# Expert gate and up weights read as runs of consecutive rows, with token features and router weights permuted to match

## The reference, cut to what matters

```
m = rmsnorm(h[:, LEAD_PAD:], g_ffn[layer])              # the token rows, width 1024
grp = argmax(softmax(m @ w_rg + b_rg))                  # 4 groups
top_val, top_idx = top_k((m @ w_re + b_re)[grp], 2)     # 2 of the 8 experts of the group
for every (token, expert e) chosen:
    hb = silu(xb @ w_gate[e]) * (xb @ w_up[e])          # 1024 -> 512, 32 experts
    y  = (hb @ w_down[e]) * gate                        # 512 -> 1024
```

## Time and profile before

| | |
|---|---|
| Median of the runs | 2676.31 us |
| Profiled execution, first to last instruction | 2682.0 us (nothing around the span is recorded) |
| TensorE busy, of the span | 2241.3 us (84%) |
| VectorE, ScalarE, GpSimd busy | 1577.4, 1063.9, 433.0 us |
| Mean granted TensorE clock | 0.872 |
| DMA | 346.55 MB in 251273 packets |

### The profile page before, as it was taken

How to read it: one execution, slowest core, us unless ns; L and a number is a source line. 1 busy time by engine, 2 the same in 40 slices (tenths; PEclk the granted TensorE clock), 3 DMA queues, 4 the chain that set the end, 5 groups by cost and what they waited for, 6 DMA issues and landing times. The chain is left out here.

```text
span 2682.0 us, 27601 instructions
## 1 busy us (share of the span) xinstructions
PE 2241.3 (84%) x10272; PEld 1841.8 (69%) x10272; DVE 1577.4 (59%) x1629; ACT 1063.9 (40%) x1243; POOL 433.0 (16%) x310
## 2 busy tenths in 40 slices
PE   6998966757999999992897787886488986899997
PEld 5885655656777787772776677765467865688786
DVE  4114578356788788884249999999733244333312
ACT  3224531215677676773243324433343222322211
POOL 0002121001111111110134454343300011000000
PEclk9996557858999999996798988888689998899999
DMA  4210000407999999984232222222023221333321
GB/s 144 73 48 1 1 0 1 167 32 248 324 342 361 333 356 365 357 316 145 51 95 78 64 63 79 79 63 64 0 89 84 94 94 32 87 95 96 107 79 63
DMA packets 251273, 346.55 MB, mean 129 GB/s; under 512 B 13951, under 2 KB 149623, under 8 KB 250151
## 3 DMA queue, kind: packets, MB, share of 16 engines
q1 hardware_dynamic: 240432, 332.49, 37.3%
q0 software_dynamic: 5200, 8.40, 1.0%
q10 hardware_dynamic: 5543, 4.34, 0.5%
HBM read 341.19 MB, written 12.65 MB: 132 GB/s over the span
## 5 line engine op out<-in xcount | busy, mean ns | idle before, releaser
L1335 DVE TENSOR_TENSOR wlo_e<-raw_e,whi_e 128x2048 fp32r<-128x2048 f32 x192 | 432.1, 2292 | 83.6 <-ACT whi_e L1269 83.6
L47 PE MATMUL pall<-hT_hi,w_lo 128*128 128x512 f32 x864 | 354.7, 411 | 53.2 <-DVE yT L2181 33.6
L1646 ACT CAST w_hi<-w_raw 128x2048 fp32r<-128x2048 f32 x89 | 169.5, 1904 | 540.9 <-PE pall L49 540.9
L1654 DVE TENSOR_TENSOR w_lo<-w_raw,w_hi 128x2048 fp32r<-128x2048 f32 x75 | 171.8, 2291 | 352.6 <-ACT w_hi L1646 352.6
L1269 ACT CAST whi_e<-raw_e 128x2048 fp32r<-128x2048 f32 x192 | 357.2, 1914 | 0.0
L48 PE MATMUL pall<-hT_lo,w_hi 128*128 128x512 f32 x864 | 348.1, 403 | 0.0
L49 PE MATMUL pall<-hT_hi,w_hi 128*128 128x512 f32 x864 | 346.5, 401 | 0.0
L2193 DVE SCALAR_TENSOR_TENSOR mixed<-yT,cols,mixed 128x512 f32<-128x512 f32 x240 | 251.2, 1047 | 7.6
L47 PEld LDWEIGHTS pall<-hT_hi,w_lo 128*128 128x128 f32 x864 | 170.4, 197 | 93.5 <-DVE yT L2181 36.4
L47 PE MATMUL pall<-whi_e,xT_lo 128*128 128x512 f32 x512 | 204.6, 400 | 9.6 <-DVE wlo_e L1335 9.6
L49 PE MATMUL pall<-whi_e,xT_hi 128*128 128x512 f32 x512 | 201.2, 393 | 0.0
(11 more groups left out here) (443 smaller groups left out, 4440.0 us busy)
## 6 DMA issues: line engine op xcount, KB each, us to landing
raw_e<-in_w_expert_up_dram SPq DMA_DIRECT2D x64, 1024.0 KB, 8.2
raw_e<-in_w_expert_down_dram SPq DMA_DIRECT2D x64, 1024.0 KB, 7.6
raw_e<-in_w_expert_gate_dram SPq DMA_DIRECT2D x64, 1024.0 KB, 7.1
w_raw<-in_w_in_dram SPq DMA_DIRECT2D x80, 512.0 KB, 5.4
w_raw<-in_w_gate_up_dram SPq DMA_DIRECT2D x44, 512.0 KB, 5.1
w_raw<-in_w_down_dram SPq DMA_DIRECT2D x22, 512.0 KB, 3.9
mixed<-in_w_in_dram SPq DMA_DIRECT2D x10, 1024.0 KB, 5.0
A<-acs_rows SPq DMA_DIRECT2D x8, 1024.0 KB, 4.9
```

What stands on the lines that cost most here:

```text
L47: nc.tensor.matmul(out, w_lo, m_hi, start=start, stop=False)
L1335: ins = nc.vector.tensor_tensor(wlo[j][:, :], raw[j][:, :], whi[j][:, :].bitcast(F32), ALU.subtract)
L1646: self.nc.scalar.copy(self.hi[i][:, :], self.raw[i][:, :]).then_inc(self.s_hi, 1)
L1654: (engine or self.nc.vector).tensor_tensor(self.lo[i][:, :], self.raw[i][:, :], self.hi[i][:, :].bitcast(F32), ALU.subtract).then_inc(self ...
```

## The change: what it does

Gate and up weights are seen as (p k) f: feature row 8p+k lies on partition p. A unit is half of what a partition holds of the matrix: four consecutive rows, one run of 8 KB. The load of a unit is still one DMA of 1 MB with the same issuer, the same wait and the same place in the program. To match, `xn` is written with its columns in the order k-major (column k*128+p of `xn` is feature 8p+k), so `m_rows`, `xg` and the transposes hold permuted features, and the router weights `wr` are loaded as (p k) c. The overflow block gets the same layout.

The core of the diff (in the third block, the gate and up loads are written in the same way):

```diff
-    w_gate = dram["w_expert_gate"][0].rearrange("e (k p) f -> p e k f", p=P)
-    w_up = dram["w_expert_up"][0].rearrange("e (k p) f -> p e k f", p=P)
+    w_gate = dram["w_expert_gate"][0].rearrange("e (p k) f -> p e (k f)", p=P)
+    w_up = dram["w_expert_up"][0].rearrange("e (p k) f -> p e (k f)", p=P)
     def unit_source(e, j):
         if j < 4:
             w = w_gate if j < 2 else w_up
-            k = 4 * (j % 2)
-            return w[:, bass.ds(e, 1), k:k + 4, :].rearrange("p o k f -> p (o k) f")
+            c = UNIT * (j % 2)
+            return w[:, bass.ds(e, 1), c:c + UNIT].rearrange("p o f -> p (o f)")
     def load(sp, j, of):
-        place = raw_e[j][:, :].rearrange("p (k c) -> p k c", k=4 if j < 4 else 2)
+        place = raw_e[j][:, :] if j < 4 else raw_e[j][:, :].rearrange("p (k c) -> p k c", k=2)
-            act.dma_start(wr[:, :, N_GROUPS:NR], dram["w_router_expert"][0].rearrange("(k p) c -> p k c", p=P)).then_inc(s["wr"], 16)
+            act.dma_start(wr[:, :, N_GROUPS:NR], dram["w_router_expert"][0].rearrange("(p k) c -> p k c", p=P)).then_inc(s["wr"], 16)
+            def fanned(t):
+                return t.rearrange("p (q k) -> p k q", k=KD)
+            def strips(t):
+                return t.rearrange("p (k q) -> p k q", k=KD)
-                nc.vector.scalar_tensor_tensor(xn[i % 2][:, :], h[:, i, :], rs[:, i:i + 1], gbc[:, :], ALU.mult,
-                                               ALU.mult).then_inc(s["xn"], 1)
+                nc.vector.scalar_tensor_tensor(strips(xn[i % 2][:, :]), fanned(h[:, i, :]), rs[:, i:i + 1], fanned(gbc[:, :]),
+                                               ALU.mult, ALU.mult).then_inc(s["xn"], 1)
```

More of the change, by code:

```diff
@@ L961, in _ @@
             act.dma_start(gbc[:, :], dram["g_ffn"][0].partition_broadcast(P)).then_inc(s["gbc"], 16)
-            act.dma_start(wr[:, :, 0:N_GROUPS], dram["w_router_group"][0].rearrange("(k p) c -> p k c", p=P)).then_inc(s["wr"], 16)
-            act.dma_start(wr[:, :, N_GROUPS:NR], dram["w_router_expert"][0].rearrange("(k p) c -> p k c", p=P)).then_inc(s["wr"], 16)
+            act.dma_start(wr[:, :, 0:N_GROUPS], dram["w_router_group"][0].rearrange("(p k) c -> p k c", p=P)).then_inc(s["wr"], 16)
+            act.dma_start(wr[:, :, N_GROUPS:NR], dram["w_router_expert"][0].rearrange("(p k) c -> p k c", p=P)).then_inc(s["wr"], 16)
             act.dma_start(rb[:, 0:N_GROUPS], dram["b_router_group"][0].partition_broadcast(P)).then_inc(s["rb"], 16)
@@ L1520, in turn @@
                 e = sp.value_load(over_e[0:1, bass.ds(j, 1)] if later(j) else over_e[0:1, 0:1], min_val=0, max_val=N_EXPERTS - 1)
-                for w, t in ((w_gate, wg), (w_up, wu), (w_down, wd)):
-                    sp.dma_start(t[:, :, :], w[:, bass.ds(e, 1), :, :].rearrange("p o k f -> p (o k) f")).then_inc(s["w"], 16)
+                for w, t in ((w_gate, wg), (w_up, wu)):
+                    sp.dma_start(t[:, :, :].rearrange("p k f -> p (k f)"),
+                                 w[:, bass.ds(e, 1), :].rearrange("p o f -> p (o f)")).then_inc(s["w"], 16)
+                sp.dma_start(wd[:, :, :], w_down[:, bass.ds(e, 1), :, :].rearrange("p o k f -> p (o k) f")).then_inc(s["w"], 16)
             blocks(sp, turn)
```

## The result

The changed kernel took 2690.11 us (median of four runs, 2689.75 to 2692.58), the kernel before 2676.58 us beside it: a ratio of 1.0052, 95% interval 1.0038 to 1.0067. It is slower by 13.5 us between the medians, and by 13.9 us going by the ratio. The forecast was slower by 32 us. The direction and the place were right, the size was not.

A forecast was written before the change was run, and what follows sets the result against it. The prediction took the late landing of the gather, which TensorE waits for, to bound the expert loop. Span 2682.0 + 31 (gather) + 1 (xn) = 2714 us, less 5.7 to the median: 2708 us, range 2658 to 2767.

The forecast's parts named there:

- What bounds the loop: Expert loop: TensorE waits for the late gather into xg, 24.4 us in 33 waits before the transposes; weights arrive early.
- the order doesn't mend this: GpSimd's order in the expert loop: gap and next gather issue both hang on TensorE's fixed work, so a late gather stays late.
- The gather behind larger packets: Expert loop: five gather packets per engine each wait for a larger weight packet, 1.13 us a turn, +31 us in all.
- The scatter: Expert loop: issued 1.2 us ahead, its five packets were taken to be out of the gather's way.
- The rival with the sooner gather: Expert loop: DMA engine load falls 1.5 us a turn, gather lands 0.5 us sooner, 2663 us; chance 0.30.
- xn: Token rows: four strided VectorE instructions of 1.286 us get slower, 0 to 2.8 us exposed, taken as 1 us.
- The worst rival: Expert loop: gather and scatter both pushed, landing 2.26 us later, lower clock with it, 2767 us; chance 0.15.
- The clock: Expert loop: longer gaps could bring stretches at 0.50 clock; no lower clock counted in the forecast.
- Signs named in advance: Expert loop: about 49,000 fewer packets, gather landing 9.0 us, transpose waits near 55 us, DMA share below 0.95.

## Why the prediction was wrong in size and right in place

**What bounds the loop** was right. The gather is late and nothing else is: taking it off the path gave 20.4 us between the medians of that chip. Of the 24.4 us of waits before, 8.9 are left there, 0.3 at a time. But "the order doesn't mend this" holds only as long as the scatter goes first. Two lines moved in GpSimd's program mend all of it.

**The gather behind larger packets** is the step that failed. It had five packets with 0.226 us each, 1.13 us a turn and 31 us in all. The packet size alone, measured on the same bytes, moves the landing by 0.7 us (7.6 to 8.3), and the time by 0.0061 to 0.0064, 16 to 17 us. The term was 1.6 times too large in the landing and nearly twice in the time. Both of its factors were off:

- A gather of 80 packets and 0.16 MB can't hold 64 rows of 4 KB, which are 0.26 MB. It holds 40 rows and 40 tiny packets; in the loop it is 32 rows in the mean (58 gathers and scatters with 4640 packets and 7.58 MB). So of the five packets of an engine two carry a row, in the mean (32 rows over 16 engines).
- A packet of 8 KB costs 0.268 us more than one of 2 KB in the loop (0.364 against 0.096), not 0.226, which took 0.317 us from tile A at a DMA share of 55.4%.

At 0.268 us for one, 0.7 us are two to three packets held up instead of five (an estimate). Which of them were held up no run shows.

**The scatter** was said to be out of the way when the gather comes. It is not: going second costs some 1.6 us of landing. The cost of larger packets didn't double by it, though. Ten turns would have been 2.26 us, and it is 0.7.

**The rival with the sooner gather** had two premises. Less load on the engines is 2% for each byte, not 9%, and it explains little here. The other, that turn-taking can't be the whole delay of 4.0 us, fits the records: ten turns of 0.096 us are 1 us, and more than half of the delay lies before the gather's first packet. Rows side by side in a unit do land the gather sooner where a unit is every second row (7.2 us instead of 7.9 with the same packets). For the halves of the changed kernel this isn't shown: with 2 KB packets the landing is 7.6, but the waits of the weight loads before the transposes are those of before, and the time is 0.9988 with an interval past 1.

```profile
PEld pall L1439 <- issue: 25.7, 31, 4.0
```

So the sum is 16 to 17 us from the packets and 1 from xn, and a gain of some 4 us from the layout, which is no more than the noise, to the 13.5 us measured. The two profiles by themselves give 29 x 0.4 = 12 us from the landing, or 8.3 from the waits; the profile of before took 7 us more than its median, so either can be too small. Why the choice of rows counts no run shows.

**The worst rival** (2.26 us, with the clock) did not come. The landing rose by 0.4 us, and the longest gap was 3.8 us against 3.6. The gap of 3.25 us from which this rival took its price was not a late landing in the main: that gather landed after 8.3 us, 0.4 above the median, but it was issued 2.1 us late, behind a scatter instruction of 3.04 us instead of 0.92.

**xn** was right: 2.108 us instead of 1.286, 0.8 us more. From its first instruction to the first gather it is 66.7 us before and 67.8 after, 1.1 us more. The two kernels with the gather first differ by 1.8 us, within the intervals.

**The clock**: counted at nothing, and the mean granted clock is 0.873 against 0.872.

**Signs named in advance**: the packets came out as said (49152 fewer). The landing was to be 9.0 us and is 8.3; the waits were to be 55 us and are 32.7. The DMA share was to be below 0.95 and is 0.96 in 700 to 1190 us, as the packets of 8 KB are less cheap than thought. The weights were to land a little sooner: up units do (8.3 to 7.9 us), gate units don't (7.1 to 7.3).

## What to carry to other kernels

Where a small DMA that someone waits for runs beside a bulk stream, the size of the stream's packets is paid by the small one: here larger runs made the bulk loads 2% cheaper for each byte and the kernel 0.5% slower. First look at what the small DMA is queued behind in its issuer's program. Moving the scatter one turn back in GpSimd's order took the gather off the path, gave 0.8%, and made the question of the packet size void. Before you multiply a cost by a count of packets, check the count against the bytes of the same row. And where two effects of a change have opposite signs, add them; don't give each a chance of its own.

## What was not expected of the hardware

Which rows a 1 MB load takes from a matrix in HBM moved the landing of another queue's DMA at the same packet size of 2 KB: 7.9 us (rows 128 apart on a partition), 7.6 (halves of 16 KB), 7.2 (every second row, and 512 consecutive rows). The 0.7 us between the first and the last are shown in the time too (0.9964 and 0.9966); the step from 7.9 to 7.6 is not. The cause is open.

In two to five turns of a profile the instruction of an indirect DMA takes about 3 us instead of 0.92, as at 714.24, and the turn is longer by 3 to 5 us. With the gather first it still does once (at 654.08, 2.96 us), and the turn stays at 17.9 us. Before has three such turns in its profile and the changed kernel two, and they hold the longest gaps of either. The slowest profile of the study against its own median (2686.27 against 2679.29 us) has five. That they make a good part of the spread of the runs is likely, but not shown. What brings them on is open.
